# Where the staging of queries and keys and the split of weights stand in an attention's steps

## The reference, cut to what matters

```python
def forgetting_attention(h, w_in, b_f, w_out):
    proj = h @ w_in
    q, k, v, f_logit = jnp.split(proj, [D_MODEL, 2 * D_MODEL, 3 * D_MODEL], axis=-1)
    ...
    log_f = jax.nn.log_sigmoid(f_logit.astype(F32) + b_f.astype(F32))
    c = jnp.cumsum(log_f, axis=1).transpose(0, 2, 1)
    ...
        logits = jnp.einsum('bhqd,bhkd->bhqk', q_b, k) * scale
        logits = logits + c_b[..., :, None] - c[..., None, :]
        ...
        p = jax.nn.softmax(jnp.where(mask, logits, -jnp.inf), axis=-1)
        return jnp.einsum('bhqk,bhkd->bhqd', p, v)
    ...
    return out @ w_out
```

## Time and profile before

| | |
|---|---|
| runs | 3992.02, 3997.28, 3998.29 us, median 3997.28 |
| profiled execution | 3999.34 us, of which its span 3997.6 us |
| mean granted clock of TensorE | 0.949 of 2.4 GHz |
| busy share of the span | PE 92%, weight loads 72%, DVE 52%, ACT 27%, POOL 27% |
| first attention, first logits to the first matmul of the next projection | 96.48 to 300.80 us |
| the same, second attention | 1909.48 to 2113.27 us |

### The profile page before, as it was taken

One profiled execution on the slowest core, in us unless ns is written; L12 is line 12 of the kernel. 1 busy time (PEld: TensorE's weight loads), 2 busy tenths in 40 slices (PEclk: granted clock), 3 DMA queues, 4 the chain that ended last, 5 costly groups with the idle time before them and its releaser, 6 DMA issues. The chain is left out here.

```text
span 3997.6 us, 44371 instructions
## 1 busy us (share of the span) xinstructions
PE 3683.6 (92%) x16819; PEld 2874.8 (72%) x16819; DVE 2068.0 (52%) x2631; ACT 1080.4 (27%) x1480; POOL 1069.7 (27%) x835
## 2 busy tenths in 40 slices
PE   7889999968999979999889999997899999779999
PEld 6667888846788848887666888762678877357887
DVE  4446554795544475444445545655543346454334
ACT  3442121123212122213442212333222223332121
POOL 0443634610554236340342635001200000130000
PEclk9889999978999989999889999987999999889999
DMA  3105444123444324442113444210133321013332
GB/s 103 48 27 127 129 124 116 58 66 75 125 131 129 107 81 131 125 116 83 44 32 100 127 127 119 81 35 21 43 95 100 88 82 56 21 32 84 93 101 79
DMA packets 554319, 346.08 MB, mean 87 GB/s; under 512 B 33270, under 2 KB 535420, under 8 KB 554172
## 3 DMA queue, kind: packets, MB, share of 16 engines
q1 hardware_dynamic: 540348, 293.79, 26.1%
q0 software_dynamic: 13824, 50.34, 4.3%
HBM read 341.01 MB, written 3.08 MB: 86 GB/s over the span
## 5 line engine op out<-in xcount | busy, mean ns | idle before, releaser
L1273 PE MATMUL ps<-h_hi,w_hi 128*128 128x512 f32 x2880 | 1154.2, 401 | 50.9 <-DVE qk L1840 17.8
L1274 PE MATMUL ps<-h_lo,w_hi 128*128 128x512 f32 x2880 | 1136.7, 395 | 0.0
L1275 PE MATMUL ps<-h_hi,w_lo 128*128 128x512 f32 x2880 | 1135.6, 394 | 0.0
L1235 DVE TENSOR_TENSOR w_lo<-w,w_hi 128x2048 fp32r<-128x2048 f32 (+2 forms) x294 | 663.4, 2257 | 168.0 <-ACT w_hi L1228 165.9
L1228 ACT ACTIVATE w_hi<-w 128x2048 fp32r<-128x2048 f32 (+2 forms) x294 | 507.0, 1725 | 708.4 <-PE ps L1275 635.1
L1273 PEld LDWEIGHTS ps<-h_hi,w_hi 128*128 128x128 f32 x2880 | 551.1, 191 | 172.3 <-issue 56.2
L1275 PEld LDWEIGHTS ps<-h_hi,w_lo 128*128 128x128 f32 x2880 | 549.6, 191 | 117.7
L1274 PEld LDWEIGHTS ps<-h_lo,w_hi 128*128 128x128 f32 x2880 | 551.4, 191 | 110.7 <-issue 0.5
L1364 DVE TENSOR_TENSOR sg<-sg,ps 128x512 f32<-128x512 f32 x132 | 90.8, 688 | 719.3 <-ACT sg L1349 719.3
L1273 PE MATMUL ps<-a_hi,w_hi 128*128 128x512 f32 x1056 | 412.0, 390 | 0.0
L1275 PE MATMUL ps<-a_hi,w_lo 128*128 128x512 f32 x1056 | 411.0, 389 | 0.0
(11 more groups left out here) (471 smaller groups left out, 3990.1 us busy)
## 6 DMA issues: line engine op xcount, KB each, us to landing
w<-in_ffn_w_gate_up SPq DMA_DIRECT2D x176, 512.0 KB
w<-in_w_ada POOLq DMA_DIRECT2D x96, 512.0 KB, 6.9
w<-in_ffn_w_down SPq DMA_DIRECT2D x64, 704.0 KB
w<-in_w_gate_up SPq DMA_DIRECT2D x88, 512.0 KB
w<-in_w_down SPq DMA_DIRECT2D x32, 704.0 KB
w<-in_fox_w_in SPq DMA_DIRECT2D x32, 512.0 KB
w<-in_w_in SPq DMA_DIRECT2D x14, 1024.0 KB
w<-in_fox_w_in SPq DMA_DIRECT2D x8, 1024.0 KB
```

Of the source, the lines that this page charges most:

```text
L1235: last = nc.vector.tensor_tensor(lo, raw, hi.bitcast(F32), ALU.subtract)
L1273: nc.tensor.matmul(out, hi, a[0][:, k, :], start=k == 0, stop=False)
L1274: nc.tensor.matmul(out, hi, a[1][:, k, :], start=False, stop=False)
L1275: return nc.tensor.matmul(out, lo, a[0][:, k, :], start=False, stop=k == kt - 1)
```

## The change

Three orders change, and nothing else. Both heads of the next pair are staged in the odd step: on ACT behind blocks 1 and 2, on DVE behind blocks 2 and 3, on POOL behind blocks 0 and 2 (for pair 0 both are staged ahead of the first step, before the first split of weights). The split of weights stands in the even step, on ACT behind block 2 and on DVE behind block 3. PE's pieces of projection in the even step are 0 behind block 1, 1 and 2 behind block 2, 3 behind block 3.

```diff
@@ tensor
-            self.project(e, p, () if even else (6, 7))
+            self.project(e, p, (0,) if even else (6, 7))
...
-            self.project(e, p, (0, 1) if even else ())
+            self.project(e, p, (1, 2) if even else ())
...
-            self.project(e, p, (2, 3) if even else ())
+            self.project(e, p, (3,) if even else ())
@@ scalar
         self.stage_high(e, 0)
+        self.stage_high(e, 1)
         self.ahead(e, 0, "scalar")
...
-                if t == 0:
-                    if s >= 2:
-                        self.turned(e, s - 2, copy, 1)
-                    if s % 2 == 0:
-                        self.stage_high(e, s + 1)
-                if s % 2 and p < self.n:
-                    if t == 1:
-                        self.ahead(e, p, "scalar")
-                        self.stage_high(e, s + 1)
+                if t == 0 and s >= 2:
+                    self.turned(e, s - 2, copy, 1)
+                if t == 2 and s % 2 == 0 and p < self.n:
+                    self.ahead(e, p, "scalar")
+                if t in (1, 2) and s % 2 and p < self.n:
+                    self.stage_high(e, s + t)
@@ gpsimd
-            if s % 2 and t % 2 and s + 1 < self.heads:
+            if s % 2 and t in (0, 2) and s + 1 < self.heads:
                 e.wait_ge(m.sem["p_scaled"], m.at("p_scaled", i + 1))
-                if t == 1:
-                    self.stage_gate(e, s + 1)
-                if t == 3:
-                    self.stage_gate(e, s + 2)
+                self.stage_gate(e, s + 1 + t // 2)
@@ vector
         self.stage_low(e, 0)
+        self.stage_low(e, 1)
         self.ahead(e, 0, "vector")
...
-                if t == 0:
-                    if s >= 2:
-                        self.turned(e, s - 2, copy, 0)
-                        self.turned(e, s - 2, copy, 2)
-                    if s % 2 == 0:
-                        self.stage_low(e, s + 1)
-                if s % 2 and p < self.n:
-                    if t == 1:
-                        self.ahead(e, p, "vector")
-                    if t == 2:
-                        self.stage_low(e, s + 1)
+                if t == 0 and s >= 2:
+                    self.turned(e, s - 2, copy, 0)
+                    self.turned(e, s - 2, copy, 2)
+                if t == 3 and s % 2 == 0 and p < self.n:
+                    self.ahead(e, p, "vector")
+                if t in (2, 3) and s % 2 and p < self.n:
+                    self.stage_low(e, s + t - 1)
```

## The result

The changed kernel takes 3923.48 us (median of 4 runs, 3913.95 to 3926.31), the kernel before 3994.65 us in the same comparison (4 runs, 3987.78 to 3998.29). The ratio is 0.9822, with a 95% interval of 0.9807 to 0.9837: 71 us, 1.8% faster. The profiled execution took 3926.31 us, its span is 3924.5 us. The forecast was 3925 us, 3908 to 3956, faster.

What follows compares the result with a forecast made beforehand. PE was taken to bound the kernel, with 5.8 of 25.1 us a pair waiting and low clock. Savings 27.1 + 6.4 + 3.4 = 36.9 per attention, twice 73.8, gave 3925 us; range 3908 to 3940, with rivals to 3956.

Steps and rivals of the forecast that it cites:

- the three waits: PE's stands in the even head's step, before its first logits, turning and projection: 1.08, 0.95, 1.49 us; 3.5 together.
- pairs: Five steady pairs of heads per attention, each falling from 25.11 to 19.7 us: 27.1 us saved.
- start: From an attention's first logits to its second odd step: 6.4 us saved, bounds 4 and 8.4.
- end: From the last odd step with projection to the next odd step, 19.06 us: 3.4 saved, bounds 2 and 4.5.
- L1: Even head's logits of query block 1, forecast at 11.3 us after the odd head's first logits, waiting 0.2 us.
- first P: First projection matmul of the next pair in the even step, forecast at 11.6 us; its 1.49 us wait gone.
- T0: First turning of the previous head's weights, in the even step: forecast at 13.4 us, some 0.4 us wait left.
- L0 of O: First logits of the odd head's step (O), where the period starts; the next one forecast at 19.7 us.
- (a): Rival: PE's clock still falls once in each pair, 2.4 us, 12 times, giving 3954 us; chance 0.13.
- (b): Rival: the two stagings on ACT become the new wait, 2 us more a pair, giving 3949 us; chance 0.12.
- (c): Rival: nothing gained, something else such as the even step's chain of maxima and copies fills 25 us; 3997 us; chance 0.03.
- (d): Rival: slower, w_lo waits for late weights with the odd step's maximum 0 behind it; 4037 us; chance 0.03.

Runs made afterwards that it cites:

- split alone (1): Kernel before, with only the split of weights moved to the even step (staging and PE's order as before): 3975.8 us, ratio 0.9963.
- staging alone (2): Changed kernel with the split back in the odd step and PE's order of before, leaving only early staging: 3987.42 us, ratio 0.9985.
- staging and PE's order (5): Changed kernel with the split of weights back in the odd step, staging and PE's new order kept: 3948.13 us, ratio 0.9884.
- staging and split (3): Changed kernel with PE's projection order of before, staging and split as changed: 3948.08 us, ratio 0.9896.
- Experiment 4: Kernel before, with unused filler matmuls within two of PE's three waits in even steps from the third pair on: 3977.8 us, ratio 0.9966.
- Experiments 6 and 7: Changed kernel with 3 (6) or 8 (7) additional unused DVE reductions behind each even-step w_lo: 3922.06 us, ratio 0.9826, and 3958.32 us, ratio 0.9915.
- the tenth: Changed kernel with each attention's first split ahead of the first staging, and DVE's output copy moved behind the next even step's turned copies: 3912.32 us, ratio 0.9794.
- the eleventh: Changed kernel with each attention's first split ahead of the first staging, and 6 filler matmuls in the last even step: 3911.54 us, ratio 0.9798.

## Why the prediction was right, point by point

The mechanism held: the three waits shrank as the walk through the streams said, from 3.5 us a pair to about 0.5, and the clock came back. That the total came out 1.5 us from the forecast is luck in part: executions of the changed kernel alone spread over 12 us (3913.95 to 3926.31). The saving is 71 us by the medians of one comparison, for 73.8 forecast; in the first attention of the profiles it is 37.6 us for 36.9, and there the terms erred both ways (pairs 0.5 less, start 1.3 more, end 0.1 less). The forecast's own upper end, 3940, isn't added up from terms: 27.1 with the lower bounds 4 and 2, twice, would have given 3931.

| | a pair, us | less than 25.11 |
|---|---|---|
| split alone (1) | 23.34 | 1.8 |
| staging alone (2) | 24.52 | 0.6 |
| staging and PE's order (5) | 21.59 | 3.5 |
| staging and split (3) | 21.77 | 3.3 |
| all three (the change) | 19.79 | 5.3 |

**What bounds a pair.** The reading that 5.8 of 25.1 us was waiting and low clock held: 5.3 are gone. Experiment 4 shows how they divide, 2.0 of clock (by its one profile) and 3.3 of waits.

**The parts support each other.** Neither of the two parts that ran alone gives half. PE's new order was not run alone, nor with the split moved and the staging left as before, so its own worth is known only on top of the other two (2.0 us). The prediction had not priced the parts one by one; its walk through ACT and DVE took them together, and its times held: L1 at 11.3 us (178.40 - 167.01 = 11.4), first P at 11.6 (11.8), T0 at 13.4 (13.5), L0 of O at 19.7 (19.8). The term of 5 pairs was 27.1 us; it measured 26.6 (125.57 - 98.96).

**The start.** Forecast 6.4 us. First L0 to first O was 15.67 us and is 13.99, from there to the next O 25.33 and 19.33: 7.7. The mis-sized term is the low clock of 1.7 us that I put into the second of these: the first profile has none, the second has it (20.96 us). The forecast of that stretch, 20.8 us (19.1 + 1.7), stands against 19.33 and 20.96: the estimate describes one of two outcomes that both occur.

**The end.** Forecast 3.4 us, with the stretch behind it unchanged. It measured 2.25 (19.06 - 16.81) and 1.03 behind it in the first profile, and 3.1 (19.06 - 15.93) in the second, where the clock stayed up. So the schedule held, and the first profile had low clock in the last even step (T0 to the next L0 3.28 us for 2.2). T0 itself came at 13.5 us for 13.4: PE's wait of 1.57 us ahead of it was in the forecast, a low clock behind it was not.

**The splits cost nothing**, as said, and the cover was 3.7 us, not 3.3. Experiments 6 and 7 bracket it: 2 us more were free, 5.7 us more made a wait of 2.04.

**DVE beside POOL.** The 0.54 us that w_lo could have lost didn't come: it takes 2.27 us. POOL lost instead: the scaling of 384 columns takes 3.20 us beside w_lo and 1.24 alone; w_lo began first. The cover held that too. (The bound of 6.5 us counted 12 splits; there are 14, which would be 7.6.) The rule of the Trainium skill, "SBUF — State Buffer", section "Who interferes with whom", that I drew on names the meeting rightly, and the scaling's 3.20 us for 1.24 agree with it; the rows add the price here.

**The rivals.** (a), a clock that still falls in each pair, is refuted: 1.00 over ten steady pairs, with turns and short logits in a row for 5 us. The rule on transposes of the Trainium skill, "TensorE: Matmul & The Clock Gate", Part 4, therefore didn't decide this case: with 20 of them in each pair, among other matmuls, the clock stayed at 1.00. (b), staging as the new wait, exists at 0.15 us; experiments 2 and 5, where the split stands in that chain, show it at 1.2 us. (c) and (d) had nothing in their favour; experiment 7 shows how (d) would have looked from 3.7 us on.

Of the expectations of experiments the first was wrong: 24.4 to 24.7 us a pair for 23.34. I took the clock to fall behind any two waits; it falls behind them in some pairs only. The total of the tenth was missed too (3903 to 3909 for 3912.32), with its pair right, that of the eleventh by 0.5 us (3908 to 3911 for 3911.54), and the saving of the fourth fell short (14 us for 16 to 24).

## What to carry to other kernels

Where each engine works strictly in order, write down for one period when each operation can start, on every engine, before moving one: here early staging and the moved split were worth 0.6 and 1.8 us alone and 5.3 together with PE's new order, because each removed a wait that the others would have exposed. Put long work without a near deadline (a split of weights) behind the last operation that the bottleneck waits for, and check its cover by adding work until it shows. And put bottleneck work that is ready where a wait can't be removed: six matmuls ahead of T0 were worth 2 us.

## What the runs showed of the hardware that I had not expected

A wait on PE costs more than itself, which I had expected: with the same waits filled by useless matmuls a pair went from 25.11 to 23.12 us. What I had not: whether the clock falls behind a given wait differs between executions: 20.96 us at 0.92 and 19.33 at 1.00 for the same stretch of the same kernel.

When a VectorE subtraction of two SBUF operands (2.27 us) and a GpSimd scaling met, the one that began second became slower: with VectorE 0.2 us ahead the scaling took 3.20 us for 1.24 and the subtraction kept its time, at 14 meetings. With another GpSimd instruction already running the subtraction took 2.83 us. No run varied the order alone.
